# Where matmul operands start in SBUF: full-length products at 64 modulo 256 bytes, block products' weights at 128

## The chip, the cores and the metric

The kernel runs on one core of one Trainium2 chip. The metric is the device time of one execution in microseconds. The kernel before took 2535.02 us, the median of three runs (2534.54 to 2538.68).

## The reference, cut to what matters

A first block (RMS norm, pooling mixer, gated linear attention, a two-level mixture of experts) is followed by a second block of two layers. Each of these layers is a feed-forward network, a hybrid attention mixer and another feed-forward network:

```
def swiglu(x, w_gate, w_up, w_down):
    return (jax.nn.silu(x @ w_gate) * (x @ w_up)) @ w_down

for l in range(DEPTH_2):                       # 2 layers, T = 512 tokens, D = 1024, D_FF = 2816
    x = x + 0.5 * swiglu(rms_norm(x, norm_ffn1[l]), ffn1_w_gate[l], ffn1_w_up[l], ffn1_w_down[l])
    x = x + hybrid_mixer(rms_norm(x, norm_mix[l]), w_in[l], ...)
    x = x + 0.5 * swiglu(rms_norm(x, norm_ffn2[l]), ffn2_w_gate[l], ffn2_w_up[l], ffn2_w_down[l])
```

All is float32. The four feed-forward networks hold most of the arithmetic.

## The kernel before, in words

Everything is kept feature-major: a tensor of 1024 features by 512 tokens lies as 128 partitions by 8 chunks by 512 columns of 4 bytes. A float32 product is made of three float32r products. Each operand is split into a rounded part (`_hi`, written by ACT) and the rest (`_lo`, written by DVE), and TensorE adds hi*hi, hi*lo and lo*hi into one PSUM bank. A weight panel is 1024 rows by 128 columns, 4096 bytes of each partition. SP fetches it into a ring (`w_raw`), ACT rounds it into `w_hi` (`round_panel`, L517), DVE takes the rest into `w_lo` (`rest_of_panel`, L522); both of these are rings of three places.

A **full-length product** (`product`, L566) takes one panel as stationary operand, chunk by chunk, and moves 512 columns past it: 8 chunks of 3 matmuls, each with its own weight load. The moving operand is `xg_hi`/`xg_lo` (the normalised x), `hid_hi`/`hid_lo` (the hidden layer), `y_hi`/`y_lo` (mixer output) or another of that kind.

A **block product** takes the place of the gate and the up product of one hidden panel j. The 2x2 blocks of weights and x are multiplied with seven half-size products in place of eight (`seven_pe`, L1922). Each of the seven is a `piece` (L1897): 4 chunks of 3 matmuls of 256 columns, all recorded at L1900. So a block is 84 matmuls, in this order: A11 B11 and A12 B21 (moving `xg`, weights in `w_hi`/`w_lo`), S2 T2, S3 T3 and S1 T1 (moving `xs`, the sums of x; weights `ws`, the sums of weights), A22 T4 (moving `xs`, weights of the up panel in the second half of a place of the ring), S4 B22 (moving `xg`, weights `ws`). Thus 36 of the 84 matmuls move `xg` and 48 move `xs`. There are 71 such blocks: runs of 5 or 8 in the first and second group of hidden panels and of 6 in the third (three runs of 5, four of 8, four of 6; the first feed-forward network has no blocks in its first group). After each run come the 8 full-length down products of the group.

Work on the vector side for one block is written out in `seven_dve` (L2206). DVE adds up weight sums (L2162), takes the rests of the panels (L522) and of the weight sums (L2129, after ACT's rounding at L2040), joins the seven results out of PSUM (L2173, L2180, L2188, L2194), and makes the hidden value and its rest (L2197, L2203, L654). For S2, S3, S1 and S4 TensorE waits for L2129's rest (`ws_low`); the first down product waits, at the chunk of the last block, for L654's rest (`split_lo`).

**Where tensors start.** Tensors are laid out one behind the other, each start rounded up to 32 bytes; the first one (`x`) starts at byte 16512 of a partition, which is 128 modulo 256. Most sizes are multiples of 256, and a few unused tensors (`before_spent`, `behind_weight`, `before_xs` and others) fill up the rest. The starts before, modulo 256: `xg_hi`, `xg_lo`, `hid_*`, `y_*`, `heads_*`, `w_raw`, `w_hi`, `w_lo`, `ws_raw`, `ws_hi`, `ws_lo`, the experts' `xt_*` and `ht_*`: 128. `xs_hi` and `xs_lo`: 64. Chunks of 2048 bytes, places of 4096 and weight blocks of 512 are multiples of 256, so every matmul of such a product has the same two values. Only `in_hi`/`in_lo` (the 528-token input of the first block) have chunks of 2112 bytes, so that their starts run through 192, 0, 64 and 128 with the weights at 128.

Of the kernel before, what the change touches and what calls it, by code (L numbers as in the profile page):

```python
# [8 lines left out]
F32R = mybir.dt.float32r  # L9
# [7 lines left out]
P = 128  # L17
# [12 lines left out]
ROUTES = N_GROUPS + N_EXPERTS  # L30
# [20 lines left out]
SPLIT = 3  # L51
# [5 lines left out]
SEVEN = {f"ff{f}_{l}": [j for j in range(3, sum(FF_GROUPS))  # L57
                        if (f, l) != (1, 0) or j >= FF_GROUPS[0]] for f in (1, 2) for l in range(DEPTH_2)}
PANEL = DC * P


def matrix_panels(rows, cols, k_groups=None, width=P):
# [97 lines left out]
def build(nc, dram, out, counts, final):  # L160
# [3 lines left out]
    stack = ExitStack()  # L164
    with stack:
        def sb(where, name, shape, dt=F32):
            return where.enter_context(nc.sbuf_tensor(name, shape, dt))
# [23 lines left out]
            return banks.tiles[b]  # L191


        x = sb(stack, "x", [P, DC, T])
        with ExitStack() as opening:
            in_hi = sb(opening, "in_hi", [P, DC, L], F32R)
# [5 lines left out]
        squares = sb(stack, "squares", [P, 2, T])  # L202
        square_sum = sb(stack, "square_sum", [P, T])
        w_raw = sb(stack, "w_raw", [P, RAW, PANEL])
        w_hi = sb(stack, "w_hi", [P, SPLIT, PANEL], F32R)
        w_lo = sb(stack, "w_lo", [P, SPLIT, PANEL], F32R)
        n_gain = 3 + 3 * DEPTH_2 + 1
        gains = sb(stack, "gains", [P, n_gain * DC])
        eps_col = sb(stack, "eps_col", [P, 1])
        eps_square = sb(stack, "eps_square", [P, 1])  # L210
        router_bias = sb(stack, "router_bias", [P, ROUTES])
        warm = sb(stack, "warm", [P, 1])
        ident = sb(stack, "ident", [P, P])
        ones = sb(stack, "ones", [P, P])
        strict = sb(stack, "strict", [P, P])
        suffix = sb(stack, "suffix", [P, P])
        minus = sb(stack, "minus", [P, P])
        ident_bf = sb(stack, "ident_bf", [P, P], BF16)
        masks_f = sb(stack, "masks_bf", [P, P], BF16)
        suffix_r = sb(stack, "suffix_r", [P, P], F32R)  # L220
# [4 lines left out]
        with ExitStack() as phase:  # L225
            meta = sb(phase, "meta", [P, DC, META])
            meta_square = sb(phase, "meta_sq", [P, DC, META])
            meta_sum = sb(phase, "meta_sum", [P, META])
            all_rstd = sb(phase, "all_rstd", [P, L])
            meta_g = sb(phase, "meta_g", [P, DC, META])  # L230
            gate_up = sb(phase, "gate_up", [GATE_RANK, 256])
            vecs = sb(phase, "vecs", [P, 2 + 4 + 1])
            pool_w = sb(phase, "pool_w", [P, 4, P])
            resets = sb(phase, "resets", [P, L])
            gla_mask = sb(phase, "gla_mask", [P, T], I32)
            y1_hi = sb(phase, "y1_hi", [P, DC, T], F32R)
            y1_lo = sb(phase, "y1_lo", [P, DC, T], F32R)
            g_low = sb(phase, "g_low", [GATE_RANK, L])
            k_f = sb(phase, "k_f", [P, 2, L])
            q_f = sb(phase, "q_f", [P, 2, T])  # L240
            v_f = sb(phase, "v_f", [P, 2, L])
            v_meta = sb(phase, "v_meta", [META, 512])
            la = sb(phase, "la", [P, 2, L])
            e1 = sb(phase, "e1", [P, L])
            bsum = sb(phase, "bsum", [P, 2, L])
            k_end = sb(phase, "k_end", [P, 2, L])
            ke_tok = sb(phase, "ke_tok", [P, TB, 256])
            ke_meta = sb(phase, "ke_meta", [META, 256])
            decay = sb(phase, "decay", [P, 2, N_CHUNK])
            carry = sb(phase, "carry", [P, 2, N_CHUNK, GLA_V])  # L250
            scores = sb(phase, "scores", [P, 2, T])
            pool_u = sb(phase, "pool_u", [P, L])
            pool_s = sb(phase, "pool_s", [P, 2, L])
            with ExitStack() as heads:
                v_tok = sb(heads, "v_tok", [P, TB, 512])

            route_parts = sb(phase, "route_parts", [P, 2, PANEL], F32R)

        head_o, head_square, head_rstd, head_r = k_end[:, :, 0:T], e1[:, 0:T], v_f[:, 0, 0:T], bsum[:, :, 0:T]


        gain_pair = sb(stack, "gain_pair", [P, 2 * DC])
        sb(stack, "before_spent", [P, 40])
        with ExitStack() as phase:

            weight_diag = sb(phase, "weight_diag", [P, TB, TOP_K, P])
# [6 lines left out]
        with ExitStack() as phase:  # L273
# [4 lines left out]
            with ExitStack() as ring:  # L278
                expert_raw = sb(ring, "expert_raw", [P, EXPERT_OWN, PANEL])
                with ExitStack() as routing:  # L280
# [48 lines left out]
            with ExitStack() as stage:  # L329
                o_raw = sb(stage, "o_raw", [P, 2, PANEL])  # L330
                o_hi = sb(stage, "o_hi", [P, 2, PANEL], F32R)
# [7 lines left out]
        with ExitStack() as phase:  # L339
            hid_hi = sb(phase, "hid_hi_ff", [P, 8, T], F32R)  # L340
            hid_lo = sb(phase, "hid_lo_ff", [P, 8, T], F32R)

            worked = sb(phase, "worked_ff", [P, 6, T // 2])
            val = sb(phase, "val_ff", [P, T])

            sb(phase, "before_xs", [P, 48])
            xs_hi = sb(phase, "xs_hi", [P, 4, DC // 2, T // 2], F32R)
            xs_lo = sb(phase, "xs_lo", [P, 4, DC // 2, T // 2], F32R)
            sb(phase, "behind_xs", [P, 16])
            up_raw = sb(phase, "up_raw", [P, UP_RAW, PANEL // 2])  # L350
            ws_raw = sb(phase, "ws_raw", [P, 6, PANEL // 2])
            with ExitStack() as early:
                x_scratch = sb(early, "x_scratch", [P, DC, T])
            ws_hi = sb(phase, "ws_hi", [P, 4, PANEL // 2], F32R)
            ws_lo = sb(phase, "ws_lo", [P, 4, PANEL // 2], F32R)
        with ExitStack() as phase:
# [31 lines left out]
        def by_seven(i):  # L388

            name, j = order[i]  # L390
            if name[0:2] == "ff" and name[4:-2] in ("gate", "up"):
                stage = name[0:3] + name[-2:]
                if j in SEVEN[stage]:
                    return stage, j, name[4:-2]
            return None
# [15 lines left out]
        ring_of, split_before, n_split, split_panels = {}, {}, 0, []  # L411
# [11 lines left out]
        def panel_shape(i):  # L423
            name, j = order[i]
            if name == "experts":
                return DC, P
            r, n_rows, c, cols = matrices[name][j]
            return n_rows // P, cols
# [11 lines left out]
        def split_memory(i):  # L440

            kc, cols = panel_shape(i)
            if order[i][0] == "route":
                return route_parts[:, 0, 0:kc * cols], route_parts[:, 1, 0:kc * cols]
            if order[i][0] in ("proj_sb_0", "proj_sb_1"):

                return xg_hi[:, order[i][1], 0:kc * cols], xg_lo[:, order[i][1], 0:kc * cols]
            if slot_of_panel[i][0] == "up":
                return w_hi[:, ring_of[i], PANEL // 2:], w_lo[:, ring_of[i], PANEL // 2:]
            return w_hi[:, ring_of[i], 0:kc * cols], w_lo[:, ring_of[i], 0:kc * cols]  # L450


# [2633 lines left out]
```

## Time and profile before

| | |
|---|---|
| median of three runs | 2535.02 us |
| the profiled execution, its own time | 2537.55 us |
| its span, first to last instruction | 2535.6 us |
| PE busy | 2441.4 us (96%) |
| DVE busy | 1704.2 us (67%) |
| ACT busy | 1129.7 us (45%) |
| mean granted TensorE clock | 0.989 |

"Busy" is the time covered by an instruction of that engine. Matmuls overlap in the records (one of 512 columns is shown 0.39 us long, and the next one starts 0.23 us after it began), so the time of a product is read from start to start. An "idle before" names who released the instruction.

### The profile page before, as it was taken

Reading aid. Unit: us, or ns where it says so; the run is one execution under the profiler, and the core shown is the slowest. Engines: PE = TensorE matmul, PEld = TensorE weight load, DVE = VectorE, ACT = ScalarE, POOL = GpSimd, SP = SyncE. Lnnn points to the kernel's source line nnn. Section 1 sums busy time; section 2 is a strip of 40 time slices with the busy share of each in tenths; the row PEclk is TensorE's granted clock in tenths of the full one; section 3 lists DMA queues with packets and bytes.
Section 4 is the critical chain, followed back from the end, with each engine's and each line's share of the span. In section 5 each row is a group of like instructions: output and inputs, shape, how many; then the busy total and the mean of one; then the engine's idle time right before and its main releaser. Section 6 shows DMA issues by size and latency. Waiting matters only on the chain. (4 is left out here: it accounts for less than half of the span.)

```text
span 2535.6 us, 38480 instructions
## 1 busy us (share of the span) xinstructions
PE 2441.4 (96%) x15217; PEld 2118.9 (84%) x15217; DVE 1704.2 (67%) x2316; ACT 1129.7 (45%) x1586; POOL 421.2 (17%) x450
## 2 busy tenths in 40 slices
PE   7997997999999999999999999999999999999998
PEld 6886776889897878778898989999888887899996
DVE  5355996668686444567686878787843446687776
ACT  5344884335353233546353454444422256544443
POOL 0002111712112400012121102111050001121110
PEclk9998998999999999999999999999999999999999
DMA  4125995246544321125564546565432212465652
GB/s 146 59 67 200 390 413 210 82 134 167 148 125 132 107 75 62 55 97 159 143 162 144 130 127 169 147 160 144 120 111 87 72 43 92 131 161 147 164 141 77
DMA packets 120713, 348.69 MB, mean 138 GB/s; under 512 B 16066, under 2 KB 21074, under 8 KB 120274
## 3 DMA queue, kind: packets, MB, share of 16 engines
q1 hardware_dynamic: 81634, 245.48, 28.9%
q0 software_dynamic: 38032, 98.06, 16.5%
q8 instruction: 125, 2.05, 0.3%
q10 hardware_dynamic: 864, 2.62, 0.3%
q14 instruction: 58, 0.48, 0.1%
HBM read 331.95 MB, written 12.58 MB: 136 GB/s over the span
## 5 line engine op out<-in xcount | busy, mean ns | idle before, releaser
L522 DVE TENSOR_TENSOR w_lo<-w_raw,w_hi 128x1024 fp32r<-128x1024 f32 (+2 forms) x353 | 421.7, 1195 | 141.2 <-ACT w_hi L517 140.0
L517 ACT ACTIVATE w_hi<-w_raw 128x1024 fp32r<-128x1024 f32 (+2 forms) x353 | 352.9, 1004 | 356.5 <-PE bank_l L566 331.1
L566 PE MATMUL bank_l<-xg_hi,w_hi 128*128 128x512 f32 x872 | 345.8, 397 | 4.9 <-DVE xg_lo L629 4.8
L566 PE MATMUL bank_l<-xg_hi,w_lo 128*128 128x512 f32 x872 | 339.6, 389 | 0.0
L566 PE MATMUL bank_l<-xg_lo,w_hi 128*128 128x512 f32 x872 | 339.6, 389 | 0.0
L566 PE MATMUL bank_l<-hid_hi_ff,w_hi 128*128 128x512 f32 x704 | 275.4, 391 | 4.9 <-DVE hid_lo_ff L654 4.6
L2040 ACT ACTIVATE ws_hi<-ws_raw 128x1024 fp32r<-128x1024 f32 x142 | 150.6, 1061 | 278.1 <-DVE ws_raw L2162 156.7
L566 PE MATMUL bank_l<-hid_lo_ff,w_hi 128*128 128x512 f32 x704 | 274.1, 389 | 0.0
L566 PE MATMUL bank_l<-hid_hi_ff,w_lo 128*128 128x512 f32 x704 | 273.9, 389 | 0.0
L1900 PE MATMUL bank_s<-xs_hi,ws_hi 128*128 128x256 f32 x852 | 237.9, 279 | 3.1 <-DVE ws_lo L2129 2.6
L1900 PE MATMUL bank_s<-xs_lo,ws_hi 128*128 128x256 f32 x852 | 235.8, 277 | 0.0
L1900 PE MATMUL bank_s<-xs_hi,ws_lo 128*128 128x256 f32 x852 | 235.5, 276 | 0.0
L2129 DVE TENSOR_TENSOR ws_lo<-ws_raw,ws_hi 128x1024 fp32r<-128x1024 f32 x142 | 173.9, 1225 | 49.9 <-ACT ws_hi L2040 42.9
L566 PEld LDWEIGHTS bank_l<-xg_hi,w_hi 128*128 128x128 f32 x872 | 163.7, 188 | 43.9 <-DVE xg_lo L629 6.0
L566 PEld LDWEIGHTS bank_l<-xg_hi,w_lo 128*128 128x128 f32 x872 | 163.7, 188 | 34.5
L566 PEld LDWEIGHTS bank_l<-xg_lo,w_hi 128*128 128x128 f32 x872 | 163.8, 188 | 34.0 <-issue 1.4
L1900 PEld LDWEIGHTS bank_s<-xs_hi,ws_hi 128*128 128x128 f32 x852 | 160.2, 188 | 6.2 <-DVE ws_lo L2129 6.1
L566 PEld LDWEIGHTS bank_l<-hid_hi_ff,w_hi 128*128 128x128 f32 x704 | 132.2, 188 | 36.5 <-DVE hid_lo_ff L654 9.7
L2289 DVE TENSOR_TENSOR val_ff<-bank_l,rstd 128x512 f32<-128x512 f32 x96 | 66.1, 689 | 140.1 <-PE bank_l L566 117.2
L1900 PEld LDWEIGHTS bank_s<-xs_lo,ws_hi 128*128 128x128 f32 x852 | 160.3, 188 | 0.0
L1900 PEld LDWEIGHTS bank_s<-xs_hi,ws_lo 128*128 128x128 f32 x852 | 160.1, 188 | 0.0
L566 PEld LDWEIGHTS bank_l<-hid_hi_ff,w_lo 128*128 128x128 f32 x704 | 132.2, 188 | 27.6
(460 smaller groups left out, 5695.1 us busy)
## 6 DMA issues: line engine op xcount, KB each, us to landing
ws_raw<-in_ff_up POOLq DMA_DIRECT2D x213, 256.0 KB, 4.1
w_raw<-in_ff_gate SPq DMA_DIRECT2D x88, 512.0 KB, 4.2
expert_raw<-in_experts SPq DMA_DIRECT2D x81, 512.0 KB, 18.8
w_raw<-in_in SPq DMA_DIRECT2D x80, 512.0 KB, 3.5
w_raw<-in_ff_down SPq DMA_DIRECT2D x64, 512.0 KB, 4.5
ws_raw<-in_ff_gate POOLq DMA_DIRECT2D x71, 256.0 KB, 5.4
up_raw<-in_ff_up SPq DMA_DIRECT2D x71, 256.0 KB, 3.0
w_raw<-in_out SPq DMA_DIRECT2D x24, 512.0 KB, 3.5
```

Source lines behind the costliest of these rows:

```text
L517: act.activation(split_memory(i)[0], split_part(i), ACT.Copy).then_inc(*panel_hi.done(i))
L522: dve.tensor_tensor(lo, split_part(i), hi.bitcast(F32), ALU.subtract).then_inc(*panel_lo.done(i))
L566: done = pe.matmul(dst, w[:, c * cols:(c + 1) * cols], moving, start=c == 0 and n == 0, stop=c == kc - 1 and n == 2)
L1900: done = pe.matmul(product_at[name], w[:, c * P:(c + 1) * P], m[:, c, :], start=c == 0 and n == 0, stop=c == DC // 2 - 1 and n == 2)
L2040: act.activation(ws_hi[:, 2 * pair:2 * pair + 2, :], raw_of_two(stage, j, pair), ACT.Copy).then_inc(*ws_high.done((stage, j, pair)))
L2129: dve.tensor_tensor(ws_lo[:, both, :], raw_of_two(stage, j, pair), ws_hi[:, both, :].bitcast(F32), ALU.subtract).then_inc(*ws_low.done((st ...
L2289: dve.tensor_tensor(val[:, :], l_banks.of(key)[:, :], rstd[:, :], ALU.mult).then_inc(*shaped.done((stage, g, m)))
```

## The change

No instruction is added, removed, reordered or given another wait. Only starts move.

- `before_x` (192 bytes) is put ahead of `x`, so `x`, `xg_*`, `w_raw`, `w_hi`, `w_lo` start at 64 modulo 256. `before_y1` (128 bytes) does the same for `y1_*`, and `before_spent` shrinks from 160 to 32 bytes, so that `hid_*`, `y_*`, `heads_*`, `xt_*`, `ht_*` and the rest behind it start at 64.
- The pads around `xs_*` go; `xs_*` stay at 64. A pad of 64 bytes (`before_ws`) ahead of `ws_hi` keeps `ws_hi` and `ws_lo` at 128.
- A place of the split rings grows from 4096 to 4352 bytes (17 times 256). The panels of block products are written and read 64 bytes into it, at 128 modulo 256; all other panels at its start, at 64.
- `strict`, `suffix`, `minus`, `router_bias` and `warm` move behind `route_parts`, in memory that only the first stages use, which pays for the larger rings.
- So for each pair (moving operand, weights of the next load): full-length products go from (128, 128) to (64, 64); pieces that move `xg` from (128, 128) to (64, 128); pieces that move `xs` stay at (64, 128); the first block's `in_*` products keep the difference of the two and change both. Some small matmuls change as well, `ident` and the attention's `suffix_r` and `minus_r` going to 192.

```diff
+SHIFT = 16
...
+        sb(stack, "before_x", [P, 48])
         x = sb(stack, "x", [P, DC, T])
...
-        w_hi = sb(stack, "w_hi", [P, SPLIT, PANEL], F32R)
-        w_lo = sb(stack, "w_lo", [P, SPLIT, PANEL], F32R)
+        w_hi = sb(stack, "w_hi", [P, SPLIT, PANEL + 64], F32R)
+        w_lo = sb(stack, "w_lo", [P, SPLIT, PANEL + 64], F32R)
...
+            sb(phase, "before_y1", [P, 32])
             y1_hi = sb(phase, "y1_hi", [P, DC, T], F32R)
...
             route_parts = sb(phase, "route_parts", [P, 2, PANEL], F32R)
+            strict = sb(phase, "strict", [P, P])
+            router_bias = sb(phase, "router_bias", [P, ROUTES])
+            warm = sb(phase, "warm", [P, 1])
+            suffix = sb(phase, "suffix", [P, P])
+            minus = sb(phase, "minus", [P, P])
...
-        sb(stack, "before_spent", [P, 40])
+        sb(stack, "before_spent", [P, 8])
...
-            sb(phase, "before_xs", [P, 48])
             xs_hi = sb(phase, "xs_hi", [P, 4, DC // 2, T // 2], F32R)
             xs_lo = sb(phase, "xs_lo", [P, 4, DC // 2, T // 2], F32R)
-            sb(phase, "behind_xs", [P, 16])
...
+            sb(phase, "before_ws", [P, SHIFT])
             ws_hi = sb(phase, "ws_hi", [P, 4, PANEL // 2], F32R)
...
             if slot_of_panel[i][0] == "up":
-                return w_hi[:, ring_of[i], PANEL // 2:], w_lo[:, ring_of[i], PANEL // 2:]
+                at = slice(PANEL // 2 + SHIFT, PANEL + SHIFT)
+                return w_hi[:, ring_of[i], at], w_lo[:, ring_of[i], at]
+            if by_seven(i):
+                at = slice(SHIFT, PANEL + SHIFT)
+                return w_hi[:, ring_of[i], at], w_lo[:, ring_of[i], at]
             return w_hi[:, ring_of[i], 0:kc * cols], w_lo[:, ring_of[i], 0:kc * cols]
```

## Rows read from the trace of the kernel before

**Rows 1.** The page, part 1: busy time by engine, share of the span, instructions.

```profile
PE 2441.4 (96%) x15217; PEld 2118.9 (84%) x15217; DVE 1704.2 (67%) x2316; ACT 1129.7 (45%) x1586; POOL 421.2 (17%) x450
```

**Rows 2.** Matmul groups by line: names, shapes, xcount | busy us, mean ns | idle.

```profile
L566 PE MATMUL bank_l<-xg_hi,w_hi 128*128 128x512 f32 x872 | 345.8, 397 | 4.9 <-DVE xg_lo L629 4.8
L566 PE MATMUL bank_l<-hid_hi_ff,w_hi 128*128 128x512 f32 x704 | 275.4, 391 | 4.9 <-DVE hid_lo_ff L654 4.6
...
L1900 PE MATMUL bank_s<-xs_hi,ws_hi 128*128 128x256 f32 x852 | 237.9, 279 | 3.1 <-DVE ws_lo L2129 2.6
...
L1900 PE MATMUL bank_t<-xg_hi,w_lo 128*128 128x256 f32 x284 | 80.4, 283 | 0.0
...
L566 PE MATMUL bank_l<-y_hi,w_hi 128*128 128x512 f32 x176 | 69.0, 392 | 0.9 <-DVE y_lo L654 0.7 <-DVE x L636 0.2
```

**Rows 3.** Timeline of PE, full-length products (start us, us, engine, line, operation).

```profile
799.65 0.39 PE L566 MATMUL bank_l<-xg_hi,w_lo 128*128 128x512 f32 x1
...
811.89 0.39 PE L566 MATMUL bank_l<-xg_hi,w_lo 128*128 128x512 f32 x1
```

**Rows 4.** Timeline of PE, one block product of a run of six.

```profile
706.72 0.28 PE L1900 MATMUL bank_t<-xg_hi,w_hi 128*128 128x256 f32 x1
...
709.60 0.29 PE L1900 MATMUL bank_s<-xs_hi,ws_hi 128*128 128x256 f32 x1
...
709.96 0.28 PE L1900 MATMUL bank_s<-xs_hi,ws_hi 128*128 128x256 f32 x1
...
715.06 0.28 PE L1900 MATMUL bank_t<-xg_hi,ws_hi 128*128 128x256 f32 x1
```

**Rows 5.** Timeline of PE, first block's full-length product, chunks 4, 5 and 7.

```profile
85.17 0.39 PE L566 MATMUL bank_l<-in_hi,w_hi 128*128 128x512 f32 x1
...
85.85 0.39 PE L566 MATMUL bank_l<-in_hi,w_hi 128*128 128x512 f32 x1
...
87.25 0.39 PE L566 MATMUL bank_l<-in_hi,w_hi 128*128 128x512 f32 x1
```

**Rows 6.** Windows, a run of six: window, length, busy PE, PEld, DVE, ACT, POOL.

```profile
697.00:755.50 58.50, 58.50 (x505) 58.50 (x504) 53.63 (x73) 28.88 (x42) 11.17 (x15) 1.00 0.53 134
```

**Rows 7.** Timeline of DVE, the last two blocks of a run of eight.

```profile
633.73 1.23 DVE L2129 TENSOR_TENSOR ws_lo<-ws_raw,ws_hi 128x1024 fp32r<-128x1024 f32 x1 [0.58 <-ACT ws_hi L2040]
...
643.88 1.23 DVE L2129 TENSOR_TENSOR ws_lo<-ws_raw,ws_hi 128x1024 fp32r<-128x1024 f32 x1 [0.57 <-ACT ws_hi L2040]
...
654.03 0.41 DVE L2194 TENSOR_TENSOR worked_ff<-bank_t,worked_ff 128x256 f32<-128x256 f32 x1
```

**Rows 8.** The waits of PE, one line of them: us in total, times, longest.

```profile
PE bank_s L1900 <- DVE ws_lo L2129: 2.6, 7, 0.5
```

**Rows 9.** Timeline of DVE, first block of a run of six, then its end.

```profile
701.52 0.69 DVE L2173 TENSOR_TENSOR worked_ff<-bank_s,worked_ff 128x512 f32<-128x512 f32 x1 [0.33 <-PE bank_s L1900]
...
704.21 0.69 DVE L2180 TENSOR_TENSOR worked_ff<-bank_s,worked_ff 128x512 f32<-128x512 f32 x1 [0.80 <-PE bank_s L1900]
...
755.72 0.42 DVE L2194 TENSOR_TENSOR worked_ff<-bank_t,worked_ff 128x256 f32<-128x256 f32 x1 [0.52 <-PE bank_t L1900]
```

**Rows 10.** Lines L2180 and L2194: min/median/max ns, and idle before them (us, times).

```profile
L2180 DVE TENSOR_TENSOR worked_ff<-bank_s,worked_ff x71: 682/686/692, 581.3 to 2486.7; 128x512 f32<-128x512 f32 x71
...
  PE bank_s L1900: 6.4, 8
...
L2194 DVE TENSOR_TENSOR worked_ff<-bank_t,worked_ff x71: 414/419/425, 584.3 to 2488.6; 128x256 f32<-128x256 f32 x71
...
  PE bank_t L1900: 2.1, 4
```

**Rows 11.** Timeline of PE, the down product behind that run of six.

```profile
760.26 0.50 PE L566 MATMUL bank_l<-hid_hi_ff,w_hi 128*128 128x512 f32 x1 [1.15 <-DVE hid_lo_ff L654]
```

**Rows 12.** Lines L2135 and L2129, DVE: duration ns min/median/max.

```profile
L2135 DVE TENSOR_TENSOR xs_lo<-x_scratch,xs_hi x16: 1218/1219/1221, 521.9 to 2212.0; 128x1024 fp32r<-128x1024 f32 x16
L2129 DVE TENSOR_TENSOR ws_lo<-ws_raw,ws_hi x142: 1215/1225/1227, 567.8 to 2482.0; 128x1024 fp32r<-128x1024 f32 x142
```

More of the change, by code:

```diff
@@ L210, in build @@
         eps_square = sb(stack, "eps_square", [P, 1])
-        router_bias = sb(stack, "router_bias", [P, ROUTES])
-        warm = sb(stack, "warm", [P, 1])
         ident = sb(stack, "ident", [P, P])
         ones = sb(stack, "ones", [P, P])
-        strict = sb(stack, "strict", [P, P])
-        suffix = sb(stack, "suffix", [P, P])
-        minus = sb(stack, "minus", [P, P])
         ident_bf = sb(stack, "ident_bf", [P, P], BF16)
```

## The prediction

> **What bounds the kernel now.** I read the page's busy times first, then the matmul groups, then PE's timeline, and last DVE's. TensorE is busy for 96% of the span [rows 1], and its largest groups hardly idle [rows 2], so at first sight each nanosecond of a matmul's step (start of one to start of the next) counts. The steps are what this change can move, so I take them from start times, not from the recorded durations, which overlap.
>
> Full-length products: the two rows are 54 matmuls apart, (811.89 - 799.65)/54 = 0.2267 us a matmul [rows 3]. At 2.4 GHz, 512 columns are 0.2133 us, so a step holds 0.0133 us more than its columns.
>
> Block products: 24 matmuls that move xg take 709.60 - 706.72 = 2.88 us, 0.1200 each. Of those that move xs, 45 take 715.06 - 709.96 = 5.10 us, 0.1133 each [rows 4]. Same columns, same engine state, weights at 128 modulo 256 in both; what differs is the moving operand's start, 128 for xg and 64 for xs. 256 columns are 0.1067 us, so one pays 0.0133 and the other 0.0067 extra. The trace thus has the price of (128, 128) and of (64, 128) at 256 columns, and that of (128, 128) at 512. It has no price of (64, 64).
>
> The nearest rows to it are in the first block's product: with weights at 128, the chunk whose moving columns start at 192 takes 0.68 us for three matmuls (0.2267 each), the two chunks at 0 and 64 take 1.40 us for six (0.2333 each) [rows 5]. So at 512 columns a pair of unlike starts can cost 0.0067 us more than (128, 128), while at 256 columns the unlike pair is the cheaper one.
>
> But in the blocks PE is not alone at its limit. DVE is busy 53.63 of 58.50 us in a run of six [rows 6], and late in a run of eight its rests of the weight sums come 643.88 - 633.73 = 10.15 us apart [rows 7]. PE's own need of a block is 36 x 0.1200 + 48 x 0.1133 = 9.76 us. DVE starts a run ahead and loses 0.39 us a block; at the end of the runs of eight and five PE waits for it [rows 8]. Its 10.15 us are its own instructions plus 0.57 us in which ACT rounds the sum that DVE has just made [rows 7]; nothing in that loop waits for TensorE.
>
> **The change part by part.**
>
> *xg at 64, block weights at 128.* The 9 groups of 284 block matmuls that move xg, one of them shown [rows 2], are 2556 = 71 x 36. They get the pair that xs has now, so 0.0067 us less each: 0.24 us a block and 17.0 us if TensorE alone set the pace. It doesn't, so I follow each kind of run to the point that its down product needs, the rest of the last hidden value. PE already waits 1.15 us for that behind a run of six [rows 11]; what arrives earlier there is the gain, and it ends on DVE.
> In a run, DVE waits for a TensorE result in two places only. In the first block of the runs of six and eight it waits for S2 T2 and S1 T1 (0.33 and 0.80 us) [rows 9]; the second wait occurs 8 times in the program, 6.4 us in all, once for each such run [rows 10]. Both results lie behind 24 matmuls that move xg, so DVE comes out 24 x 0.0067 = 0.16 us earlier, and runs at 10.15 us a block from there. And in the last block of the runs of six it waits 0.52 us for S4 B22 [rows 9], 4 times in all [rows 10]. There PE comes 6 x 0.24 = 1.44 us earlier and DVE can use 0.52 + 0.16 = 0.68 us of it. At the end of a run of eight this wait is absent (the third row of [rows 7] shows no idle), so the run gets only the 0.16. A run of five begins with PE waiting for DVE and stays so: 0. Sum: 4 x 0.68 + 4 x 0.16 + 3 x 0 = 3.4 us. The other 13.6 us become longer waits of PE for L2129 and for L654. Bounds: 0 (if DVE's start doesn't follow) and 17.0 (if DVE didn't bind).
>
> *Full-length operands at 64, both.* 3 x (872 + 704 + 176) = 5256 matmuls of the feed-forward networks, the mixers' projections and the outputs [rows 2], nearly all in stretches where PE is full. Between the bounds of one step of 0.0067 us more and one less that is 35 us either way. I take 0: the two starts move together, so their difference, which is what two streams reading the same memory would collide by, remains 0. That (64, 128) helps at 256 columns fits this, and the rows cannot exclude that the start itself matters; both ends are kept.
>
> *Split rings of 4352 bytes, blocks' panels 64 bytes in.* ACT and DVE write the same number of bytes. DVE's target at 64 modulo 256 takes 1219 ns (the rest of the x sums) and at 128 takes 1225 ns [rows 12], same shape. So 0; even 6 ns on the 1.2 us of each of some 600 such instructions would be under 4 us and mostly off the path.
>
> *Small tensors moved, ident and the attention's suffix matrices at 192.* About 150 float32r matmuls of the attention get another pair; at one step of 0.0067 us, 1 us either way. I take 0. Transposes with ident step at the pace of their weight loads, and I take 0 for them too. DMA targets shift by 64 bytes with unchanged row lengths: 0, and the panels are fetched well ahead of ACT.
>
> Against the profiled execution, 2537.55 us (a span of 2535.6 and 1.95 around it), the sum is 2534.2. That execution is 2.5 us above the median of the runs; on the median, 2535.0 - 3.4 = 2531.6 us.
>
> **A rule against this.** [rows 4] show a step of 0.1200 against 0.1133 us by nothing but a start address. The Trainium skill, page "SBUF — State Buffer", section "Who interferes with whom", gives TensorE two independent read ports, one for the moving operand and one for the weight load, and says that PE never waits on anyone. By it, no address would matter, and the time would stay at 2535.0. The trace speaks against the rule at least for pairs of starts; it is rival 5 below.
>
> **Rivals.**
> 1. *The full gain* (2518.0). The blocks speed up by 0.24 us each and DVE follows. For it: only 2.6 us of waits of PE for L2129 in the whole program [rows 8]. Against it: 10.15 against 9.76 us a block [rows 7].
> 2. *(64, 64) is better than (128, 128)* at 512 columns, by one step: 35 us off beside the 3.4, 2496.6. For it: 0.0133 us of surplus in each step [rows 3] leave room, and 64 is the better moving start at 256 columns [rows 4]. Against it: that was with the other operand elsewhere.
> 3. *(64, 64) is worse, and the kernel slower.* Place: L566's 5256 matmuls. Price: 0.0067 us each, as chunks at 0 and 64 have it [rows 5], +35.0 - 3.4 = 31.6 us, 2566.6. It decides from 3.4/5256 = 0.65 ns a matmul on. For it: at 512 columns 128 is the best moving start seen and 64 one of the bad ones. Against it: there the weights stayed at 128.
> 4. *Less than I sum*: a wait of DVE for ACT or a late sum from POOL's queue eats the 0.52 us. This is inside the first case's own range.
> 5. *No address matters*: 2535.0, the two kinds of step differing for another reason, such as the order of pieces. Against it: A22 T4 takes its weights from the same ring as A12 B21, moves xs, and lies within the 45 matmuls of 0.1133 us [rows 4].
>
> **How the numbers follow.** Forecast 0.60, its own range 2528.5 to 2535. Rival 1 0.06, rival 2 0.14, rival 3 0.17, rival 5 0.03. A measurement of this kernel tells 0.2%, 5.1 us, from no change. In the forecast's case the gain passes 5.1 us one time in four: 0.15; with rivals 1 and 2, faster is 0.35. Same is 0.44 of the first case and 0.03: 0.47. Slower is rival 3 and 0.01 of the first case: 0.18. The range takes in the forecast, its bounds and rival 2 with 6 us on it, and leaves out rival 3: 2490 to 2541.
>
> **What would show it.** Steps of 0.1133 us in all seven pieces; full-length steps of 0.2267 unchanged. The idle of L2194 before PE (2.1 us) goes to 0; L2180's 6.4 shrinks; PE's waits for L2129 and for L654 grow together by some 13 us; DVE's 10.15 us between rests late in a run stays. I am wrong if a full-length step is not 0.2267, or if a run of six ends more than 0.9 us earlier than before, measured from its first matmul to the first of its down product's last chunk.

## The result, and the profile after

The changed kernel takes 2542.75 us (median of 19 runs, lowest 2539.25); the kernel before, run beside it on the same chip, 2536.44. The ratio is 1.0026, with a 95% interval of 1.0019 to 1.0033: 0.26% or 6.6 us slower. Two of the 19 runs (3284.83 and 4543.57 us) had a lower granted clock, 0.69 and 0.82; the ratio leaves them out, and the median of the other 17 is 2542.10. The prediction, 2531.6 us, had the wrong sign, and the time lies outside its range. The profiled execution of the changed kernel took 2544.28 us, with a span of 2542.3. Line numbers after the change are 6 higher than before.

The page of the changed kernel, parts 1 and 5 (line, engine, names, count | busy us, mean ns of one | idle before):

```profile
PE 2442.2 (96%) x15217; PEld 2122.7 (83%) x15217; DVE 1704.5 (67%) x2316; ACT 1129.7 (44%) x1586; POOL 421.6 (17%) x450
...
L572 PE MATMUL bank_l<-hid_hi_ff,w_hi 128*128 128x512 f32 x704 | 274.9, 390 | 5.1 <-DVE hid_lo_ff L660 4.8
...
L1906 PE MATMUL bank_s<-xs_hi,ws_hi 128*128 128x256 f32 x852 | 240.5, 282 | 4.7 <-DVE ws_lo L2135 4.6
L1906 PE MATMUL bank_s<-xs_lo,ws_hi 128*128 128x256 f32 x852 | 238.9, 280 | 0.0
```

The busy times say nothing here: PE's grew by 0.8 us [rows 1]. The group of xs_hi does: 282 ns a record where it was 279 [rows 2]. Its operands kept their starts, and yet it is the one that became slower.

The timeline of PE in the changed kernel (start us, us, engine, line, operation). First two full-length matmuls, 54 apart:

```profile
801.78 0.39 PE L572 MATMUL bank_l<-xg_hi,w_lo 128*128 128x512 f32 x1
...
814.02 0.39 PE L572 MATMUL bank_l<-xg_hi,w_lo 128*128 128x512 f32 x1
```

12.24/54 = 0.2267 us, as before [rows 3]. Then one block of the same run of six as in [rows 4]:

```profile
707.46 0.28 PE L1906 MATMUL bank_t<-xg_hi,w_hi 128*128 128x256 f32 x1
...
710.28 0.28 PE L1906 MATMUL bank_s<-xs_hi,ws_hi 128*128 128x256 f32 x1
...
715.58 0.28 PE L1906 MATMUL bank_s<-xs_hi,w_hi 128*128 128x256 f32 x1
```

24 matmuls that move xg take 2.82 us, 0.1176 each (0.1200 before); the 45 that move xs 5.30 us, 0.1178 each (0.1133 before [rows 4]). All seven pieces now have one step, but it is 117.8 ns and not the 113.3 that xs had. It is so in every run of six and of eight. In the runs of five it is different. Here is one, PE's timeline again, the last number being the idle time and its releaser:

```profile
1182.09 0.39 PE L1906 MATMUL bank_s<-xs_hi,ws_hi 128*128 128x256 f32 x1 [0.48 <-DVE ws_lo L2135]
...
1186.40 0.28 PE L1906 MATMUL bank_t<-xg_lo,w_hi 128*128 128x256 f32 x1
...
1193.88 0.28 PE L1906 MATMUL bank_s<-xs_lo,w_hi 128*128 128x256 f32 x1
```

PE has waited for DVE in the run's first block, and the 66 matmuls from 1186.40 to 1193.88 take 0.1133 us each. These are the same instructions on the same starts as in the block of 0.1178. So a pair of starts has no one price: a stream of 256-column matmuls whose moving operand starts 64 bytes below its weights keeps up one of two steps, 117.8 or 113.3 ns. Read from the start times of all block matmuls, of 497 pieces 424 stepped at 117.8 and 44 at 113.3 (29 at neither, for a wait in them or at their end).

Per block that is 84 x 0.1178 = 9.89 us against 36 x 0.1200 + 48 x 0.1133 = 9.76. The clock has no part in it; the window of [rows 6] in the changed kernel (same columns, PEclk is the number behind POOL) again has 1.00, the full 2.4 GHz, and 9 matmuls fewer:

```profile
697.00:755.50 58.50, 58.50 (x496) 58.38 (x495) 52.96 (x72) 29.01 (x42) 11.20 (x15) 1.00 0.54 135
```

DVE's idle before the lines of the prediction, in the changed kernel (the summary of a line: duration, then what ended its idle, us and times):

```profile
L2186 DVE TENSOR_TENSOR worked_ff<-bank_s,worked_ff x71: 679/683/692, 582.2 to 2493.4; 128x512 f32<-128x512 f32 x71
  PE bank_s L1906: 8.9, 16
...
L2200 DVE TENSOR_TENSOR worked_ff<-bank_t,worked_ff x71: 411/417/425, 585.1 to 2495.4; 128x256 f32<-128x256 f32 x71
  PE bank_t L1906: 3.3, 8
```

Before it was 6.4 us in 8 waits and 2.1 in 4 [rows 10]: DVE now waits for TensorE more often, as a slower TensorE has it. What this costs a run of six is read from its first matmul to its down product's first wait. PE's timeline before, then after:

```profile
696.97 0.28 PE L1900 MATMUL bank_t<-xg_hi,w_hi 128*128 128x256 f32 x1
```

```profile
697.56 0.28 PE L1906 MATMUL bank_t<-xg_hi,w_hi 128*128 128x256 f32 x1
...
761.66 0.50 PE L572 MATMUL bank_l<-hid_hi_ff,w_hi 128*128 128x512 f32 x1 [1.15 <-DVE hid_lo_ff L660]
```

Before 760.26 [rows 11] - 696.97 = 63.29 us, after 761.66 - 697.56 = 64.10: 0.81 more, which is 6 x 0.135 of the blocks. From the first block matmul of each run to the last matmul of its down product, the two traces differ so:

| runs | before, us | after, us | sum of the differences |
|---|---|---|---|
| 4 of eight blocks | 122.65, 122.21, 122.61, 121.71 | 122.47 each | +0.7 |
| 4 of six | 92.45, 92.46, 92.46, 92.48 | 93.29, 93.27, 93.27, 93.25 | +3.2 |
| 3 of five | 94.46, 94.24, 94.70 | 94.61, 95.50, 94.99 | +1.7 |

That is 5.6 of the 6.7 us between the two spans. Another 0.8 lies ahead of the first run (it begins at 574.1 us before and 574.9 after); this is no more than scatter, since the first run of e3, with the same layout up to there, begins at 572.0.

The runs of six show TensorE's own loss whole: 24 x 0.135 = 3.2 us. In the runs of eight it would be 32 x 0.135 = 4.3 us, and the traces differ by 0.7. Most of what is missing is an accident of the execution before. In three of its four runs of eight one rest of the weight sums came 0.5 to 0.95 us late, because ACT, whose rounding it needs, had waited for a transfer. ACT's timeline before, then DVE's:

```profile
621.96 0.63 ACT L2046 ACTIVATE ws_raw<-ws_raw 128x512 f32<-128x512 f32 x1 [3.13 <-DMA ws_raw<-in_ff_gate]
```

```profile
623.57 1.23 DVE L2129 TENSOR_TENSOR ws_lo<-ws_raw,ws_hi 128x1024 fp32r<-128x1024 f32 x1 [1.52 <-ACT ws_hi L2040]
627.18 1.23 DVE L2129 TENSOR_TENSOR ws_lo<-ws_raw,ws_hi 128x1024 fp32r<-128x1024 f32 x1
```

The wait is 1.52 us where it is 0.58 in [rows 7]. The fourth run of eight had no late rest, PE stepped through its blocks without a listed wait, and it took 121.71 us; the others are 0.94, 0.50 and 0.90 us longer. Such late rests come now and then in both layouts (one in e10, two in e5, none in e7), and none fell into a run of eight of the changed kernel's profiled execution.

### The profile page after: what moved, and what is told of

Read it like the earlier page. It is cut to its first block and busy times, and to the rows that moved or that the text cites. A ratio compares the mean times of both kernels' runs of the same rounds, so it can differ in the third digit from the quotient of the medians.

```text
span 2542.3 us, 38480 instructions
## 1 busy us (share of the span) xinstructions
PE 2442.2 (96%) x15217; PEld 2122.7 (83%) x15217; DVE 1704.5 (67%) x2316; ACT 1129.7 (44%) x1586; POOL 421.6 (17%) x450
## 5 line engine op out<-in xcount | busy, mean ns | idle before, releaser
L2135 DVE TENSOR_TENSOR ws_lo<-ws_raw,ws_hi 128x1024 fp32r<-128x1024 f32 x142 | 173.9, 1225 | 48.8 <-ACT ws_hi L2046 41.8
```

Source lines behind the costliest of these rows:

```text
L2135: dve.tensor_tensor(ws_lo[:, both, :], raw_of_two(stage, j, pair), ws_hi[:, both, :].bitcast(F32), ALU.subtract).then_inc(*ws_low.done((st ...
```

## The experiments

Each time is a median, and each ratio is to the kernel before on the same chip. "The step" is start to start.

**Is it the pair, the start itself, or the way in?** Four versions move starts further. In this section a pair is (moving operand, weights) modulo 256, as before.

e1 puts the gate panels of the blocks at a place's start, so A11 B11 and A12 B21 have (64, 64) and the rest (64, 128):

```diff
-            if by_seven(i):
-                at = slice(SHIFT, PANEL + SHIFT)
-                return w_hi[:, ring_of[i], at], w_lo[:, ring_of[i], at]
```

> The changed kernel, with one edit: the gate panels of block products start at 64 modulo 256 again, so A11 B11 and A12 B21 of every block run on the pair (64, 64), all other pieces on (64, 128) as in the changed kernel. Theory H (a stream of equal pairs holds the step it enters with, 117.8 or 113.3 ns, and a stretch on an equal pair of starts puts the next one into 113.3): 24 steps of 120 ns, then 60 of 113.3, 9.68 us a block where nothing waits; the kernel comes out at 2532 to 2534 us beside 2536.4 of before and 2542.8 of the changed one, since DVE's 10.15 us a block hide the rest. Theory A (the new absolute addresses of xs and ws make 117.8 ns): the 24 steps are 120, the 60 others stay at 117.8, 9.95 us a block, and the time is 2543 to 2546 us.

Measured: 2545.28 us, 1.0029 [1.0017, 1.0042]. In the runs of six and eight the two pieces on the equal pair step at 120 ns and all others at 117.8, 9.95 us a block. An equal pair ahead of the others does not bring 113.3 back where the weights' start rises between them (64 to 128) and the moving start stays.

e3 does the same in the first block of each run alone:

```diff
-            if by_seven(i):
+            if by_seven(i) and (order[i][1] - 1 in SEVEN[by_seven(i)[0]] and order[i][1] not in (8, 16)):
```

> The changed kernel, with the gate panel of only the first block of each run (11 runs) starting at 64 modulo 256. Theory H: in a run the first 24 matmuls step by 120 ns, and then every step to the end of the run is 113.3, because nothing but a wait re-rolls it: 9.52 us a block. By DVE's 10.15 us a block the gain over before is about 3.4 us: 2531.5 to 2534 us. Theory A: only the first 24 steps of a run change, all others stay at 117.8: 2542 to 2544 us.

Measured: 2543.61 us, 1.0024 [1.0013, 1.0036]. After the 24 matmuls at 120 the runs of six and eight stay at 117.8. So theory H fails here, too: a stretch on an equal pair ahead does not by itself bring 113.3.

e2 moves every operand up by 64 bytes, so no difference changes:

```diff
-        sb(stack, "before_x", [P, 48])
+        sb(stack, "before_x", [P, 64])
```

> The changed kernel with 64 more bytes ahead of x, so every tensor starts 64 bytes later: full-length products on (128, 128), block products on (128, 192). If only the difference of the two starts counts: block steps of 117.8 ns in runs of six and eight, full-length steps of 226.7, and 2541 to 2544 us. If the start itself counts (a moving operand at 128 is dearer at 256 columns): block steps of 120 ns or another value, and 2 to 4 us more.

Measured: 2542.54 us, 1.0024 [1.0014, 1.0034], the changed kernel's own ratio. xg's pieces are now on (128, 192) and step at 117.8 in the runs of six and eight; full-length products are back on (128, 128) at 0.2267. A common shift of 64 bytes changes neither step: here the difference of the two starts counts, not where they lie.

e4 puts all weight panels at 128, so the full-length products run on (64, 128):

```diff
-            return w_hi[:, ring_of[i], 0:kc * cols], w_lo[:, ring_of[i], 0:kc * cols]
+            at = slice(SHIFT, kc * cols + SHIFT)
+            return w_hi[:, ring_of[i], at], w_lo[:, ring_of[i], at]
```

> The changed kernel with all weight panels 64 bytes into their place, so full-length products run on (64, 128), too. By the first block's rows (unlike starts at 512 columns, 0.2333 against 0.2267 us) 5256 full-length steps cost 6.7 ns more: about 35 us, 2576 to 2580 us. If a stream of equal pairs holds the step that it enters with, the long runs of full-length products may hold one value below 233 ns instead, and the time is anywhere between 2500 and 2580. A block run then begins behind a product with unlike starts: by theory H it may be entered in another step than 117.8 ns.

Measured: 2571.4 us (2 runs, 2568.62 and 2574.18), 1.0136 [1.0118, 1.0155], 35 us above the kernel before, and 29 above the changed kernel, which this version edits; 2576 to 2580 had been expected. Its timeline of PE, two full-length matmuls 54 apart:

```profile
821.82 0.39 PE L573 MATMUL bank_l<-xg_lo,w_hi 128*128 128x512 f32 x1
...
834.42 0.39 PE L573 MATMUL bank_l<-xg_lo,w_hi 128*128 128x512 f32 x1
```

12.60/54 = 0.2333 us, the step of the unlike chunks in [rows 5]. The prediction's bound of one step of 0.0067 us was thus real, with 29 us in the time where 5256 matmuls make 35; it belongs to the pair (64, 128) and not to (64, 64). Why 6 us fewer arrive was not looked into, and two runs do not settle the size. In the first block's product the distance matters in the same way, though [rows 5] do not show it well. They are from the only one of six such products in which chunk 4, at 192, steps by less than 0.23 us. In the other five it takes 0.233 a matmul, as here (first matmuls of its chunks 4 and 5, PE's timeline before):

```profile
135.40 0.40 PE L566 MATMUL bank_l<-in_hi,w_hi 128*128 128x512 f32 x1
...
136.10 0.40 PE L566 MATMUL bank_l<-in_hi,w_hi 128*128 128x512 f32 x1
```

**What leads into the fast step?** e7 puts the operands ahead of a run, `hid_*` and the down panels, at 128, so that at the run's begin the moving start falls from 128 to 64 and the weights stay; the stream ahead has 512 columns:

```diff
+            sb(phase, "before_hid", [P, SHIFT])
+            sb(phase, "before_xs", [P, 48])
...
-            if by_seven(i):
-                at = slice(SHIFT, PANEL + SHIFT)
+            if by_seven(i) or "down" in order[i][0]:
+                at = slice(SHIFT, kc * cols + SHIFT)
```

> The changed kernel with hid_* and the down panels at 128 modulo 256 in place of 64, so a run of six or eight is entered from a down product on (128, 128): the moving operand's start changes to 64, the weights' start stays at 128. In the changed kernel both change and their difference goes from 0 to -64 by the weights. Theory S (the step that a stream at difference -64 holds, 113.3 or 117.8 ns, is set at its entry: 113.3 when the moving start changes, 117.8 when the weights' start does): the runs of six and eight step by 113.3 ns from the first matmul to the last or to the first wait, 9.52 us a block, and DVE's 10.15 us a block leave 2531 to 2534 us. Rival C (the entry is chance, or what matters is what lies ahead of the run by other means): they stay at 117.8 ns, and the time is that of the changed kernel, 2541 to 2544 us.

Measured: 2542.25 us, 1.0024 [1.0014, 1.0034]; 117.8 ns in the runs of six and eight. That the moving start alone falls is not enough behind a stream of 512 columns.

e8 puts A11 B11 and A12 B21 on (128, 192), xg 64 bytes below its weights, and lets both starts fall to xs's (64, 128) in every block; S4 B22 is on (128, 128):

```diff
-        sb(stack, "before_x", [P, 48])
+        sb(stack, "before_x", [P, 64])
...
+            sb(phase, "before_xs", [P, 48])
...
-                at = slice(PANEL // 2 + SHIFT, PANEL + SHIFT)
+                at = slice(PANEL // 2, PANEL)
```

> The layout of the kernel before (all at 128 modulo 256, xs at 64), with the gate panels of block products at 192, so A11 B11 and A12 B21 run at (128, 192), S2 T2 to A22 T4 at (64, 128) and S4 B22 at (128, 128). Before, the step fell from 120 to 113.3 ns where the moving start changed from 128 to 64. Here that place changes both starts and keeps their difference, and the difference -64 is entered at A11 B11 by the weights' start. Theory S: 117.8 ns from A11 B11 to A22 T4, 120 in S4 B22, 9.9 us a block, 2541 to 2545 us. Rival C (the xs pieces are fast since xs comes behind xg, or by their own addresses, which are those of before modulo 256): S2 T2 to A22 T4 stay at 113.3 ns, 9.7 us a block or less, 2531 to 2537 us.

Measured: 2535.49 us, 0.9999 [0.999, 1.0008], the time of the kernel before. That both starts fall does no harm, so the idea behind e7 was wrong too. A block of it, PE's timeline:

```profile
705.77 0.28 PE L1907 MATMUL bank_t<-xg_hi,w_hi 128*128 128x256 f32 x1
...
708.60 0.29 PE L1907 MATMUL bank_s<-xs_hi,ws_hi 128*128 128x256 f32 x1
...
709.30 0.28 PE L1907 MATMUL bank_s<-xs_hi,ws_hi 128*128 128x256 f32 x1
...
714.06 0.28 PE L1907 MATMUL bank_t<-xg_hi,ws_hi 128*128 128x256 f32 x1
```

24 steps of xg take 2.83 us (0.1179), the next six 0.70 (0.1167), and the 42 from 709.30 4.76, 0.1133 each: the stream changes over within six matmuls of the fall. The same passage is in the kernel before, in each block: three matmuls in 0.36 us and then 0.1133 [rows 4].

**The entry by itself.** What e8 and the kernel before share is a fall of the moving start inside a stream of 256 columns. e9 adds just that to the changed kernel, and moves no operand: ahead of each of the 11 runs six matmuls of 256 columns read xg from 16 columns (64 bytes) further, on the pair (128, 128), into the bank that the first piece overwrites.

```diff
+            if by_seven_first(stage, j):
+                weight = gate_half(pe, stage, j, 0)[0][:, 0:P]
+                for n in range(6):
+                    part = (xg_hi, xg_lo)[n % 2]
+                    pe.matmul(product_at["A11 B11"], weight, part[:, 0, 16:half_t + 16], start=True, stop=True)
```

> The changed kernel with six extra matmuls of 256 columns ahead of each of the 11 runs, on the pair (128, 128): the first weight block of the gate panel, and xg moved from 64 bytes further on, into the bank that A11 B11 clears next. The weights' start then stays at 128 and the moving start falls from 128 to 64, as where xs follows xg in the kernel before. Theory M (a fall of the moving start by 64 bytes within a stream of 256-column steps puts the stream into 113.3 ns, and it stays there until PE waits): every block of the runs of six and eight steps by 113.3 ns to its end or first wait, though no operand of theirs has moved. The extra 0.72 us a run make DVE start 0.56 us later than before in runs of six and eight: about 2538 to 2540 us. Rival C (nothing ahead of the run matters, or only a wait re-rolls the step): the blocks stay at 117.8 ns, and the time is the changed kernel's plus up to 8 us, 2547 to 2551 us.

Its control e10 adds the same six from xg's own start, `part[:, 0, 0:half_t + 0]`, on (64, 128):

> The control of the kernel with six extra matmuls: the same six, with xg moved from its own start, so on the pair (64, 128), with no fall of the moving start. Theory M: the blocks stay at 117.8 ns and the time is the changed kernel's plus up to 8 us, 2547 to 2551 us. Rival C in the form that any short matmuls ahead of a run re-roll the step: part of the runs are at 113.3 ns.

e12 is e9 with two matmuls in place of six, and e15 with four:

> As the kernel with six extra matmuls on (128, 128), with only two ahead of each run. Theory M: if two are enough, all blocks at 113.3 ns for 0.24 us a run; DVE then begins at most 0.08 us later than before, and the runs of six end 0.44 us earlier: 2533.5 to 2535.5 us, no slower than before. If the change of step needs a longer stretch (it took four steps where xs follows xg in the kernel before), the blocks stay at 117.8 ns and the time is 2543 to 2546 us.

> The changed kernel with four extra matmuls on (128, 128) ahead of each run; six put the stream into 113.3 ns, two did not. If four are enough, 0.24 us a run less than with six on the way to DVE's start: 2536 to 2538 us. If not, 117.8 ns and 2545 to 2548 us.

| added ahead of each run | time, us | ratio to before | pieces at 113.3 / 117.8 ns |
|---|---|---|---|
| none (the changed kernel) | 2542.75 | 1.0026 | 44 / 424 |
| six at (64, 128) | 2549.43 | 1.0057 [1.0041, 1.0073] | 59 / 413 |
| two at (128, 128) | 2545.82 | 1.0041 [1.0027, 1.0055] | 68 / 399 |
| four at (128, 128) | 2536.6 | 0.9995 [0.9987, 1.0004] | 426 / 12 |
| six at (128, 128) | 2537.95 | 1.0007 [0.9998, 1.0016] | 407 / 19 |

PE's timeline, the run of six in e9 (L1944 is the added line), then in e10:

```profile
694.35 0.28 PE L1944 MATMUL bank_t<-xg_hi,w_hi 128*128 128x256 f32 x1
...
695.06 0.29 PE L1906 MATMUL bank_t<-xg_hi,w_hi 128*128 128x256 f32 x1
...
696.10 0.28 PE L1906 MATMUL bank_t<-xg_hi,w_hi 128*128 128x256 f32 x1
...
697.80 0.28 PE L1906 MATMUL bank_s<-xs_hi,ws_hi 128*128 128x256 f32 x1
```

```profile
696.90 0.28 PE L1944 MATMUL bank_t<-xg_hi,w_hi 128*128 128x256 f32 x1
...
697.61 0.28 PE L1906 MATMUL bank_t<-xg_hi,w_hi 128*128 128x256 f32 x1
...
699.02 0.28 PE L1906 MATMUL bank_s<-xg_hi,w_hi 128*128 128x256 f32 x1
```

In e9 15 matmuls from 696.10 take 1.70 us (0.1133), in e10 12 take 1.41 (0.1175): the same matmuls on the same operands, and what ran just ahead of them decides. By the ratios, six added matmuls a run on the one pair take 4.8 us (0.19%) off the changed kernel, and the same six on the other add 7.9. The rings, the new order of the small tensors and the starts of DVE's and ACT's operands are all in e9 and e10 alike, so they do not set the step. Nor did they make DVE or ACT slower: in the changed kernel they were busy for 1704.5 and 1129.7 us, against 1704.2 and 1129.7 before [rows 1]. Two matmuls ahead are not enough, four are.

**Where TensorE's gain ends.** With 9.52 us a block in place of 9.76, e9 has 0.24 x 71 = 17 us less of TensorE in its blocks than the kernel before, and 11 x 0.72 = 7.9 us more in the added matmuls: 9.1 less in all, and the same time. Two cuts of DVE's work ask whether DVE is what binds. In e5 (the kernel before) and e6b (the changed one) the scaling of the gate value by `rstd` is done on 32 of its 512 columns only, and the rest is left out:

```diff
-            dve.tensor_tensor(gate_value, gate_value, rstd[:, :], ALU.mult).then_inc(
+            dve.tensor_tensor(gate_value[:, 0:32], gate_value[:, 0:32], rstd[:, 0:32], ALU.mult).then_inc(
```

> The kernel before, in which L2197 multiplies 32 of 512 columns of the gate value by rstd (the rest of that product is left out, in the 71 blocks). It takes some 0.6 us off DVE's 10.15 us a block. If DVE's loop is what costs the waits at the ends of the runs of five and eight (PE waits 7 times for L2129), PE's waits for L2129 fall to nearly nothing but for the first block of the runs of five, and the down products wait less: 2 to 5 us faster than before, 2531.5 to 2534.5 us. If DVE's loop doesn't bind anywhere, the time is that of before within 1 us.

> The changed kernel with the same part of L2197 left out. TensorE's 9.9 us a block (117.8 ns a step) should then be the bound: the changed kernel lost little to DVE in runs of eight and six, so it gains at most 1 to 3 us: 2540 to 2542 us, and its distance to the light kernel before is TensorE's own 0.135 us a block times 71, 8 to 10 us, against 6.6 us between the two full ones. If the changed kernel's loss lay on DVE or ACT (slower writes or reads at the new starts), the distance shrinks below 4 us.

Measured: 2531.58 us, 0.9983 [0.9974, 0.9992], and 2541.16, 1.0016 [1.0007, 1.0025]. They are 9.6 us apart, which is TensorE's own difference, 0.135 x 71 = 9.6, where with DVE's full work it was 6.6. By the ratios it is 8.4 against 6.6, and each of the three intervals is 1.8 to 2.3 us wide to either side, so these times do not show that DVE covered a part. They agree with it, and do not bear out a loss on DVE or ACT, which should have made the distance shrink.

e11 is e9 with the same cut:

> The kernel with six extra matmuls on (128, 128), with L2197's part left out as in the two light kernels (32 of 512 columns multiplied by rstd in the 71 blocks). TensorE's need is then 84 x 113.3 ns = 9.52 us a block and 0.72 us a run: 71 x 0.24 - 7.9 = 9.1 us less than the light kernel before (2531.6), 2522.5 us, if DVE (some 9.55 us a block without that part) hardly binds. By theory M with DVE binding from 9.5 us on: 2523 to 2527 us. By rival C: 2545 to 2549 us.

Measured: 2531.87 us, 0.9988 [0.9979, 0.9997], where some 2525 were expected. Its timeline of DVE late in a run of eight says why:

```profile
626.38 1.23 DVE L2140 TENSOR_TENSOR ws_lo<-ws_raw,ws_hi 128x1024 fp32r<-128x1024 f32 x1 [0.62 <-ACT ws_hi L2051]
...
636.54 1.23 DVE L2140 TENSOR_TENSOR ws_lo<-ws_raw,ws_hi 128x1024 fp32r<-128x1024 f32 x1 [0.62 <-ACT ws_hi L2051]
```

The rests still come 636.54 - 626.38 = 10.16 us apart. The freed half microsecond stands there as a wait of 0.62 us for ACT, where the kernel before has none listed (the row at 627.18 above): the cut instruction lay in the shadow of ACT's rounding, not in the loop. The same waits of 0.62 us stand in e5 and e6b, so the expectation that this cut takes 0.6 us off the 10.15 was wrong for them, too. What the cut shortened is the chain behind each run: three of the four runs of six take 91.95 us in e5, where they took 92.46 before.

So e13 (with e9's six matmuls) and e14 (the kernel before) cut an instruction that lies on no such shadow, the rest of the blocks' up panels, made for the last 32 of 512 columns only and otherwise left out:

```diff
-            dve.tensor_tensor(lo, split_part(i), hi.bitcast(F32), ALU.subtract).then_inc(*panel_lo.done(i))
+            n = PANEL // 2 - 32 if slot_of_panel[i][0] == "up" else 0
+            dve.tensor_tensor(lo[:, n:], split_part(i)[:, n:], hi[:, n:].bitcast(F32), ALU.subtract).then_inc(*panel_lo.done(i))
```

> The changed kernel with six extra matmuls on (128, 128) ahead of each run, and the rest of the up panels of block products (L522, 128x512, 71 of them) cut to its last 32 of 512 columns; the other 480 of that rest are left out. This takes some 0.6 us off the loop of DVE and ACT itself (sum, rounding, rest, sum, rounding, rest), which the light kernels did not do: there DVE just waited 0.62 us for ACT where L2197 had covered it. If that loop's 10.15 us a block is what ate the gain of TensorE's 113.3 ns steps: the loop is about 9.55 us, the late blocks of a run take 9.5 to 9.6 us in place of 10.15, and the kernel is 7 to 9 us faster than the kernel before with the same cut. If something else bounds the blocks at 10.15 us (the transfers of POOL's queue): late blocks stay at 10.15 us, and the difference is within 2 us of that between the uncut ones (+2.7).

> The kernel before with the same cut of the up panels' rests. The loop of DVE and ACT comes down from 10.15 to some 9.55 us a block, below TensorE's 9.76: no waits at the ends of the runs of five and eight, 9.76 us in all but the first blocks of the runs of five. 2 to 4 us less than before: 2531.5 to 2533.5 us. If POOL's transfers set the 10.15 us: no difference from before.

Measured: e13 2523.73 us, 0.9945 [0.9931, 0.9959]; e14 2530.83, 0.9978 [0.9967, 0.9988]. e13 is within what was expected, e14 0.7 us below it. Now the fast step is worth 7.1 us of TensorE's 9.1, where with DVE's full work it was worth nothing. DVE's timeline of e13 late in a run of eight has the loop at 642.10 - 632.44 = 9.66 us in place of 10.15, so it was this loop, and not POOL's transfers, that held the late blocks:

```profile
632.44 1.23 DVE L2141 TENSOR_TENSOR ws_lo<-ws_raw,ws_hi 128x1024 fp32r<-128x1024 f32 x1 [0.58 <-ACT ws_hi L2052]
...
642.10 1.23 DVE L2141 TENSOR_TENSOR ws_lo<-ws_raw,ws_hi 128x1024 fp32r<-128x1024 f32 x1 [0.58 <-ACT ws_hi L2052]
```

PE's waits in e9, then in e13 (us in total, times, longest):

```profile
PE bank_l L572 <- DVE hid_lo_ff L660: 6.3, 7, 1.5
...
PE bank_s L1906 <- DVE ws_lo L2140: 6.0, 16, 0.6
```

```profile
PE bank_l L573 <- DVE hid_lo_ff L661: 4.9, 6, 1.2
PE bank_s L1907 <- DVE ws_lo L2141: 1.5, 4, 0.6
```

In e9 TensorE catches up with DVE in the sixth block (once in the fifth), and from there goes at some 10.15 us a block. In e13 the blocks stay at 9.52 to the end of the runs of six and, but for one of them, of eight.

## Why the prediction was wrong

**The step that failed.** "They get the pair that xs has now, so 0.0067 us less each: 0.24 us a block." The pair did become the same, and the step did not. I had read 0.1133 us in [rows 4] as the price of (64, 128), while it was one of two steps that a stream on this pair can hold, and the kernel before led its stream into the good one anew in each block, by passing from xg at 128 to xs at 64. The change took that passage away: within a run the moving start is now 64 everywhere. So the term has two halves, and only one was in the sum. xg: 2556 matmuls, 120.0 to 117.8 ns, 5.6 us less. xs: 48 x 71 = 3408 matmuls, "stay at (64, 128)" and cost nothing by the sum, 113.3 to 117.8 ns, 15.3 us more. Together 9.7 us more of TensorE, where the sum had 17.0 less. (Some pieces of the runs of five were at 113.3, so it was a little under 9.7.)

**What DVE made of it.** That DVE's 10.15 us a block would hide most of a gain was right (e9 against e13 and e14). That it holds PE up at the end of the runs of eight before the change was read too broadly: the run of [rows 7] is one of the three with a late rest behind a transfer, and the run of eight without one had no listed wait for DVE in its blocks. So the 3.6 us of loss missing in the runs of eight are by 2.3 us luck of that execution; the other 1.3 were not traced to a cause. The places were right as well. The idle of DVE before PE at L2180 and L2194 was to shrink and grew, because TensorE became later; a run of six was to end 0.68 us earlier and ends 0.81 later. Rival 1, "the full gain", would not have come about even with fast steps in all blocks: of TensorE's net 9.1 us nothing arrives in e9 (2537.95 us, 1.0007), nor of the 11.7 in e15, which adds 5.3 us of matmuls in place of 7.9 (2536.6 us, 0.9995). The two signs of being wrong that the prediction named, another full-length step and a run of six that ends far earlier, did not come; it was the first sign of being right, 0.1133 us in all seven pieces, that failed.

**What was right.** The full-length products at nothing: 0.2267 us as before, and e2 shows that a common shift changes nothing. The kept bound of one step was the price of (64, 128) at 512 columns (e4). The rings, the splits and the small tensors at nothing: e9, which has them all, is at 1.0007 [0.9998, 1.0016], and DVE's and ACT's busy times did not move. That a small cost of theirs is hidden in e9 by its faster steps is not excluded.

**The rivals.** The one for "slower" put it at the full-length matmuls, which did not move; none of the five was what happened. Rival 5, that no address matters, is excluded by e4 and e2 together.

**What stays open.** Why there are two steps is not settled. The runs give when a stream of 256 columns on the difference of 64 enters the fast one:

| stream ahead of it | then | step held |
|---|---|---|
| 24 matmuls of 256 on (128, 128), before | (64, 128) | 113.3 |
| 24 of 256 on (128, 192), e8 | (64, 128) | 113.3 |
| 6 or 4 of 256 on (128, 128), e9, e15 | (64, 128) | 113.3 |
| 2 of 256 on (128, 128), e12 | (64, 128) | 117.8 |
| 24 of 256 on (64, 64), e1, e3 | (64, 128) | 117.8 |
| 6 of 256 on (64, 128), e10 | (64, 128) | 117.8 |
| 512 columns on (128, 128), e7 | (64, 128) | 117.8 |
| 512 columns on (64, 64), after | (64, 128) | 117.8 |
| 512 columns on (64, 128), e4 | (64, 128) | 113.3 in two of the 11 runs, 117.8 in nine |

A fall of the moving start by 64 bytes in a stream of 256 columns is common to all the fast ones but those two runs of e4, and absent from all slow ones but e12. After a wait of PE either step follows: after the one shown at 1182.09 the fast one came, after others the slow one. Even a listed wait is not needed: in e4 two streams went from 117.8 to 113.3 (near 1193.9 and 1542.9 us) behind single steps of 132 and 123 ns. And in e4 the 512-column stream ahead of a run steps by 231 and 236 ns in turn; the two runs entered behind a 236 were fast, the nine behind a 231 slow. So the fall is one way in and not the only one, and how the two reads lie in time to each other at the entry may be what counts; no version was made to show it. What in a wait decides was not tried, nor was any other fall than one of 64 bytes, nor a rise of the moving start. The one run of five that became 1.26 us longer, where the others grew by 0.15 and 0.29, is also the only one that stepped at 117.8 in its second to fourth block; whether this is the reason is not shown. No version tried, with the whole computation, beats the kernel before.

## What to carry to other kernels

A step read from a trace belongs to the stream it was read in. Before its price is given to other instructions, ask what ran ahead of them, and look for the same pair of operands elsewhere in the trace at another step; the instructions that a change leaves alone can lose what their neighbours did for them. And cost a gain on a nearly full engine by its neighbour's loop: cut an instruction of that loop in both kernels and see whether the difference between them changes.

## What the runs showed of the hardware

- Two steps for the same instructions on the same starts, 113.3 and 117.8 ns at 256 float32r columns with a weight load each, both at a granted clock of full speed (2.4 GHz); at equal starts 120.0. Each is kept until a wait of TensorE or until the starts change, but for two places in e4, where it changed behind a step only 14 and 5 ns longer than the others.
- At 512 columns equal starts cost 226.7 ns and starts 64 bytes apart, at (64, 128), 233.3 (e4): the order is the other way round than at 256. In the time it was 29 us between the changed kernel and e4.
- A common shift by 64 bytes of both operands changes neither (e2).
- The Trainium skill, page "SBUF — State Buffer", section "Who interferes with whom", gives TensorE two independent read ports for moving operand and weight load, so that their addresses should not matter. This case's runs disagree: 0.2333 us a matmul in e4 against 0.2267 in the changed kernel, by the weights' start alone, and 2571.4 against 2542.75 us, 1.1%.
